# Queries and gates of a hybrid encoder layer: the tokens' high and low parts side by side in one matmul of 512 columns

## What is computed

```python
xn = rmsnorm(h, norm_g)
z = xn @ w_in                      # 2048 -> 3*1024 + 1024 + 1024 + 1024 + 3*1024 + 1024 + 3*2048
u, x1, x2 = short_conv(hy_in)      # width 3
y_a = hyena_mixer(u, x1, x2, kf, skip) * silu(hy_gate)      # two long convolutions by FFT
y_b = fourier_mixer(fn_in) * silu(fn_gate)                  # 2-D DFT, real part
y_c = neighborhood_attention(q, k, v, rpb, meta_bias) * silu(na_gate)
m = g_a * (y_a @ w_a) + g_b * (y_b @ w_b) + g_c * (y_c @ w_c)
out = rmsnorm(h + m @ w_out, final_g)[:, 16:]
```

## Time and profile before

| | us |
|---|---|
| median of 3 runs | 1137.92 |
| lowest and highest | 1137.79, 1138.51 |
| span of the profiled execution | 1136.7 |
| PE busy in it | 1111.2 |
| DVE busy | 767.9 |
| ACT busy | 567.7 |

### The profile page before, as it was taken

The page is one execution under the profiler, slowest core; times in us unless marked ns, Lnnn a source line. Parts: engine busy times, 40 slices in busy tenths (PEclk is TensorE's granted clock), DMA queues, the critical chain, the costliest instruction groups (busy, mean ns, idle before and its releaser), DMA issues.

```text
span 1136.7 us, 17224 instructions
## 1 busy us (share of the span) xinstructions
PE 1111.2 (98%) x7158; PEld 1006.8 (89%) x7158; DVE 767.9 (68%) x1149; ACT 567.7 (50%) x787; POOL 62.0 (5%) x98
## 2 busy tenths in 40 slices
PE   4999999999999999999999999999999999999997
PEld 2999999999999999999999988888888888888886
DVE  6778887778787687886888775454555455455554
ACT  6565555556545455554554564443444444344443
POOL 4030000300001200002000000000000000000000
PEclk9999999999999999999999999999999999999999
DMA  8644443644435533435543575555555555556652
GB/s 311 236 137 168 148 149 121 203 167 149 136 125 195 185 120 141 149 121 186 186 148 117 167 262 198 195 184 192 185 185 185 189 189 183 197 200 244 242 185 111
DMA packets 30494, 201.54 MB, mean 177 GB/s; under 512 B 3873, under 2 KB 4193, under 8 KB 7745
## 3 DMA queue, kind: packets, MB, share of 16 engines
q1 hardware_dynamic: 25024, 180.16, 45.3%
q0 software_dynamic: 5248, 19.77, 5.3%
q10 hardware_dynamic: 144, 0.52, 0.1%
HBM read 195.19 MB, written 5.24 MB: 176 GB/s over the span
## 4 chain that ended last, share of the span: by engine, by line
PE 74%; DVE 15%; ACT 6%; issue 4%; DMA 0%; ACTq 0%; DVEq 0%
PE ps L570 23%; PE ps L572 23%; PE ps L571 23%; DVE w_lo L1322 4%; ACT w_hi L982 2%; DVE prod L1563 1%; DVE prod L1564 1%; PE ps L594 1%; PE ps L575 1%; DVE k_lo L1322 1%; DVE prod L1565 1%; DVE y_lo L1322 1%; DVE prod L1566 1%; DVE hm L1409 1%; ACT y_hi L1183 1%
## 5 line engine op out<-in xcount | busy, mean ns | idle before, releaser
L1322 DVE TENSOR_TENSOR w_lo<-raw,w_hi 128x1024 fp32r<-128x1024 f32 x336 | 409.1, 1230 | 267.2 <-ACT w_hi L982 266.9
L982 ACT ACTIVATE w_hi<-raw 128x1024 fp32r<-128x1024 f32 x336 | 351.2, 1056 | 349.4 <-PE ps L572 347.6
L570 PE MATMUL ps<-xn_hi,w_hi 128*128 128x272 f32 (+2 forms) x1280 | 367.6, 287 | 0.0
L571 PE MATMUL ps<-xn_lo,w_hi 128*128 128x272 f32 (+2 forms) x1280 | 365.8, 286 | 0.0
L572 PE MATMUL ps<-xn_hi,w_lo 128*128 128x272 f32 (+2 forms) x1280 | 365.4, 285 | 0.0
L570 PEld LDWEIGHTS ps<-xn_hi,w_hi 128*128 128x128 f32 x1280 | 242.3, 189 | 2.0
L571 PEld LDWEIGHTS ps<-xn_lo,w_hi 128*128 128x128 f32 x1280 | 242.1, 189 | 0.7
L572 PEld LDWEIGHTS ps<-xn_hi,w_lo 128*128 128x128 f32 x1280 | 242.3, 189 | 0.0
L570 PE MATMUL ps<-w_hi,xn_hi 128*128 128x512 f32 x384 | 152.3, 397 | 0.0
L572 PE MATMUL ps<-w_hi,xn_lo 128*128 128x512 f32 x384 | 150.9, 393 | 0.0
L571 PE MATMUL ps<-w_lo,xn_hi 128*128 128x512 f32 x384 | 150.6, 392 | 0.0
(11 more groups left out here) (257 smaller groups left out, 1333.5 us busy)
## 6 DMA issues: line engine op xcount, KB each, us to landing
raw<-w_stream SPq DMA_DIRECT2D x168, 1024.0 KB, 4.9
branch_y<-ystage POOLq DMA_DIRECT2D x12, 256.0 KB, 3.3
y_raw<-branch_y POOLq DMA_DIRECT2D x3, 1024.0 KB, 6.7
xin<-x SPq DMA_DIRECT2D x2, 1024.0 KB, 6.9
w4s<-w POOLq DMA_DIRECT2D x16, 128.0 KB, 5.9
absd<-decay POOLq DMA_DIRECT2D x8, 256.0 KB, 6.3
h<-x POOLq DMA_DIRECT2D x2, 1024.0 KB, 8.0
rows_t<-rpb POOLq DMA_DIRECT2D x8, 219.0 KB, 6.2
```

The costliest lines, as they stand in the source:

```text
L570: mm(out_ap, a_hi, b_hi, start=first, stop=False)
L571: mm(out_ap, a_hi, b_lo, start=False, stop=False)
L982: A(w_hi[:, w % 2, part, :], raw[:, w % 4, 1024 * part:1024 * part + 1024], ACT.Copy).then_inc(hi_done, 1)
L1322: return V.tensor_tensor(dst, src, hi.bitcast(F32), ALU.subtract)
```

## The change

The two tiles `xn_hi` and `xn_lo` become halves of one tile `xn_two`. For q, hgate, ngate and fgate a new `summed_slab` replaces `proj_slab`: for each k one matmul with `w_hi` stationary and both parts of the 256 tokens moving, 512 columns into a whole bank (columns 0 to 255 w_hi*xn_hi, columns 256 to 511 w_hi*xn_lo), and one with `w_lo` stationary and xn_hi moving, 256 columns added to the first half. Two matmuls take the place of three. When the block ends, ACT copies the second half of the bank into an SBUF tile `both`, DVE adds the first half to it, and that frees the bank. What is made of the sum moves one slab on:

- q: both engines' work on `q_two` moves from step 3 to step 4, ahead of `spectra` on DVE;
- hgate: tanh and product from step 13 to step 14; ngate: from step 17 to step 18, with the product of branch c; fgate: from step 19 to step 0 of the next chunk;
- `fourier_gated` moves from step 19 to step 1 of the next chunk in chunks 1 to 3 (in chunk 0 it stands at step 1 in both).

```diff
+    xn_two = place("xn_two", [128, 2, KT, L], F32R)
+    xn_hi, xn_lo = xn_two[:, 0, :, :], xn_two[:, 1, :, :]
...
+    both = place("both", [128, 2, NG])
...
+            def summed_slab(w, bank, half):
+
+                for nt in range(2):
+                    pe.wait_ge(lo_done, 2 * w + nt + 1)
+                    for k in range(8):
+                        cols = slice(128 * k, 128 * k + 128)
+                        mm(ps[:, bank + nt, :].rearrange("p (h n) -> p h n", h=2), w_hi[:, w % 2, nt, cols],
+                           xn_two[:, :, 8 * half + k, NM:L], start=half == 0 and k == 0, stop=False)
+                        last = mm(ps[:, bank + nt, 0:NG], w_lo[:, w % 4, nt, cols], xn_hi[:, 8 * half + k, NM:L],
+                                  start=False, stop=half == 1 and k == 7)
+                    last.then_inc(half_used, 1)
...
# ACT
-                    ins = A(gate[:, :, :], src16, ACT.Tanh, scale=0.5)
+                    act.wait_ge(both_used, summed(c, name) - 1)
+                    A(both[:, :, :], ps[:, bank:bank + 2, NG:2 * NG], ACT.Copy).then_inc(half_kept, 1)
+                    return
...
+                    if t == 4:
+                        queries_high(c)
+                    if t in (14, 18):
+                        gate_tanh(c, "hgate" if t == 14 else "ngate")
+                    if t == 0:
+                        gate_tanh(c - 1, "fgate")
...
# DVE
+                if name in ("q", "hgate", "ngate", "fgate"):
+                    dve.wait_ge(half_kept, summed(c, name))
+                    V.tensor_tensor(both[:, :, :], both[:, :, :], ps[:, bank:bank + 2, 0:NG], ALU.add).then_inc(proj_read, 1)
+                    return
...
+            def gate_final(c, name):
+                dve.wait_ge(tanh_done, 3 * c + ("hgate", "ngate", "fgate").index(name) + 2)
+                V.scalar_tensor_tensor(gate[:, :, :], gate[:, :, :], 1.0, both[:, :, :], ALU.add, ALU.mult).then_inc(both_used, 1)
+                dve.wait_ge(both_used, summed(c, name))
...
-                    if t == 1 and c == 0:
-                        fourier_gated(0, 2)
+                    if t == 0:
+                        gate_final(c - 1, "fgate")
+                    if t == 1:
+                        fourier_gated(c)
                     if t == 4:
+                        queries_low(c)
                         spectra(c, (0, 1), 0)
+                    if t == 14:
+                        gate_final(c, "hgate")
...
-                    if t == 17:
+                    if t == 18:
+                        gate_final(c, "ngate")
...
-                    if t == 19 and c < LAST:
-                        fourier_gated(c + 1, blocks_read(c, "fgate"))
```

More of the change, by code:

```diff
@@ L102, in copies_made, with summed @@
 def copies_made(c, name):
-    return 1 + c * (NBLK - 2) + ("u", "q", "k", "x1", "x2", "hgate", "ngate", "fgate").index(name) + 1
+    return 4 * c + ("u", "k", "x1", "x2").index(name) + 1
+def summed(c, name):
+    return 4 * c + ("q", "hgate", "ngate", "fgate").index(name) + 2
 FPOS = np.concatenate([np.arange(256, L), np.arange(0, 256, 2), np.arange(1, 256, 2)])
@@ L803, in _ @@
                         wide_slab(slab_of(c, t), PAIR["gate", 0, 0], xn_hi, xn_lo, 4 * q, KT, NM)
+                    elif name in ("q", "hgate", "ngate", "fgate"):
+                        summed_slab(slab_of(c, t), 2 * (t // 2 % 2), t % 2)
                     else:
@@ L1128, in evac @@
                                 scale=params[:, bass.ds(c * 2 + (CW + 24 + t0 + i), 1)])
-                elif name == "q":
-                    for hh in range(HC):
-                        r = slice(64 * (hh % 2), 64 * (hh % 2) + 64)
-                        ins = A(q_two[r, hh, :].rearrange("p (r n) -> p r n", r=4),
-                                ps[r, bank + hh // 2, 0:NG].rearrange("p (r n) -> p r n", r=4)[:, :, ::-1], ACT.Copy, scale=0.125)
                 elif name == "k":
@@ L1147, in evac, with queries_high, gate_tanh @@
                 else:
[L1148 to L1154 removed]
+                    act.wait_ge(both_used, summed(c, name) - 1)
+                    A(both[:, :, :], ps[:, bank:bank + 2, NG:2 * NG], ACT.Copy).then_inc(half_kept, 1)
+                    return
+                ins.then_inc(a_ev, 1)
+            def queries_high(c):
+                act.wait_ge(proj_read, blocks_read(c, "q"))
+                for hh in range(HC):
+                    r = slice(64 * (hh % 2), 64 * (hh % 2) + 64)
+                    ins = A(q_two[r, hh, :].rearrange("p (r n) -> p r n", r=4),
+                            both[r, hh // 2, :].rearrange("p (r n) -> p r n", r=4)[:, :, ::-1], ACT.Copy, scale=0.125)
+                ins.then_inc(q_high, 1)
+            def gate_tanh(c, name):
+                act.wait_ge(proj_read, blocks_read(c, name) if c >= 0 else 2)
+                done, turns = {"hgate": (yb_done, c + 1), "ngate": (ya_done, c + 1), "fgate": (yc_done, c + 1)}[name]
+                if turns:
+                    act.wait_ge(done, turns)
+                if name == "hgate":
+                    act.wait_ge(s_mm, c * HC + HC)
+                A(gate[:, :, :], both[:, :, :], ACT.Tanh, scale=0.5).then_inc(tanh_done, 1)
             def turned(n_th, done, dst, rest, bank, ready, w=CC, twin=32):
@@ L1498, in evac @@
                 src = ps[:, bank:bank + 2, 0:L]
-                src16 = ps[:, bank:bank + 2, 0:NG]
                 if name == "v":
```

41 lines of the change are left out of this document (17 added, 24 removed).

## The result

The changed kernel takes 1156.7 us (median of 4 runs, 1156.0 to 1156.9); the kernel before took 1138.2 us in the runs beside it. The ratio is 1.0163, with a 95% interval of 1.0151 to 1.0176. So it is slower, as forecast, but by 18.5 us where 9.2 were forecast, and it lies above the range.

A forecast was written before the change was run, and what follows sets the result against it. PE was taken as the bound except where two DVE and ACT chains arrive late. Chain A 9.6, chain B 1.7 and PE -2.1 gave +9.2 us, 1147.1 us on the median of 1137.92; range 1140 to 1151.

The forecast's parts named there:

- What bounds the kernel: PE is the bound except where two chains of DVE and ACT make it wait, ahead of the scores and unfold.
- The gain on PE: Paired matmuls in q and gate slabs save 9.9 ns per contraction tile; -2.1 us where PE does not wait.
- fourier_gated and q in chain A: Added DVE and ACT work delays chain A: +0.69 us in chunks 1 to 3, +0.75 in all four.
- chain A: DVE and ACT work from step 1 to the scores after step 8; 3.19 us longer in chunks 1 to 3.
- POOL in chain A: Bias additions, now at step 1, collide with sd by turns: +1.75 us in chunks 1 to 3, bounds 0 to 2.5.
- tanh in chain B: ACT's later hgate tanh in step 14 delays unfold by 0.58 us in chunks 0 to 2, 1.7 us together.
- chain B: DVE and ACT work from the scores of step 11 to unfold, for which PE waits after step 16; +1.7 us.
- Elsewhere 0: Gate products of steps 18 and 0, branch c's later store and POOL's filter-weight loads cost 0 where PE is the bound.
- no collision: Rival: sd and make_bias pass each other or POOL starts later; +4.0 us, 1141.9 us; no or one collision, chance 0.20.
- dearer operand: Rival: 512 columns cost as much as two of 256, no PE gain; 1149.2 us; with a further wait, chance 0.13.

The follow-up runs named there:

- e1: The changed kernel with make_bias on POOL put ahead of the store of branch b; 1145.8 us, ratio 1.0070.
- e2: The kernel before with only fourier_gated of chunks 1 to 3 moved from step 19 to step 1 of the next chunk; 1151.9 us, ratio 1.0125.
- e18: The changed kernel with POOL's bias additions held until the product hm has been made; 1149.0 us, ratio 1.0100.
- e15: e2 with POOL's bias additions held until the product hm, just ahead of sd, has been made; 1143.3 us.
- e16: e2 with POOL's bias additions held until sd_lo of the same place has been made; 1147.1 us.
- e5: e1 with the tanh and product of hgate put back at step 13; 1142.1 us, ratio 1.0036.
- e12: e6 with the first branch's split put ahead of ngate's tanh and product in step 18 of the last chunk; 1134.8 us, ratio 0.9974.
- e9: e6 with each 512-column matmul split again into two of 256 columns; 1137.8 us, ratio 0.9998.
- e6: e5 with fourier_gated in step 0 of chunks 1 to 3 and the query subtractions put between the spectra's first steps; 1136.0 us, ratio 0.9983.
- e4: e1 with each 512-column matmul split again into two of 256 columns; 1146.6 us.
- e7: The changed kernel with 28 unused 256-column matmuls on PE ahead of its wait for the fold in chunks 1 to 3; 1155.7 us, ratio 1.0157.
- e8: e2 with POOL's bias additions held until the block of sd in question has been made; 1144.2 us.
- e11: e5 with fourier_gated made in step 0 of chunks 1 to 3; 1140.6 us, ratio 1.0026.

## Why the prediction was wrong in size

- **What bounds the kernel: right.** Both chains cost what was added to them. The warning against PE's 98% held: with PE's stream shorter, the time grew.
- **The gain on PE: right in kind, too large.** 9.9 ns per pair were predicted, 5 to 6 measured (2.79 instead of 2.84 us a half), since the pair takes 0.349 us and not 0.345: from the start of the 512-column matmul to the next it is 0.232 us in the median, where the merge has 0.227. Kept were 1.4 us instead of 2.1. The rows for 512 columns came from the merge, where the same kind of matmul follows; the prediction named as the bound and did not move toward it.
- **fourier_gated and q in chain A: right.** In chunk 1 PE waits 3.5 us for the fold, which is 0.69 + 3.35 less the 0.52 in hand. The two terms together were to cost 1.44 us a chunk; in e1, where no collision adds to them, they cost 1.2.
- **POOL in chain A: the step that failed.** Place, order and partner were right: `fourier_gated`, store, the four additions 0.16 us ahead of `sd`. The size was not: "`sd`'s first addition waits for POOL's first (0.95 us, 0.8 of it left), the second for POOL's second" made 1.75 us, and the trace has 3.35. With upper bound 2.5 it was outside the bounds too. The prediction took alternation from chunk 0 for a rule, where the worst case, the whole row of 3.64 us, was in the earlier trace rows. This is 1.6 x 3 = 4.8 of the 8.9 us that the span missed. e1, e2 and e18 show it by taking it away or putting it in; in e18 the row still meets `sd`, and with turns each chain A is 2.4 to 2.6 us shorter. Why this row lets DVE in only at its end, where the same row elsewhere takes turns, is open.
- The Trainium skill ("SBUF — State Buffer", "Who interferes with whom") says, of VectorE's modes that use two ports, that whoever issues first gets the shared pair for the whole instruction; it does not say who comes next. If the loser's turn is next, it waits for one addition, and in chunk 0, e15 and e16 the traces look so (0.90 to 1.97 us for an instruction of DVE, its own work included). `sd` of the changed kernel does not: it waits for four.
- **tanh in chain B: right.** 1.7 predicted, 2.1 measured; e5 took 1.5 us off the wait for `unfold`.
- **"Elsewhere 0": wrong by 1.3 us.** The same two hand-overs cost 0.4 us in step 15 of the last chunk (chain B's end, where I counted chunks 0 to 2 only) and 0.5 at the start of the merge, where the tanh of ngate now stands ahead of `yb_hi`; e12 undid the latter. q in chunk 0, taken as hidden (0 to 0.8), cost 0.35.
- **The clock: not in the prediction at all.** 1.4 us in chunk 0 and about 0.3 each in chunks 2 and 3 of the changed kernel.
- Rival "no collision" is what e1 tried: 1145.8, not 1141.9, since it still has the clock, the last chunk and the merge. Rival "dearer operand" came true in part: some 4 of the 9.9 ns are gone, and what is left still shows in e9. The range's upper end, 1151, had room for 1.3 us more of collision a chunk, not for the 1.6 of a full row.

## What to carry to other kernels

When an added hand-over delays one engine's instruction, look at what waits for it on the third engine, and price a collision at the whole row of instructions queued there, not at one of them. Work that a change adds to a busy-looking but not binding engine can be free, but only at the place where that engine waits: the same edit, with the same sums and copies, cost 18 us in the order it was given, and in another order, with POOL's row at another place, was 2 to 3 us faster than the kernel before (e6, e12). Before shortening PE's stream, find the chain that it hides.

## What the runs showed of the hardware

- A DVE addition of 0.42 us took 3.77 us beside four back-to-back POOL additions (also 4.04 for 512 elements), waiting for the last; other DVE instructions with two SBUF inputs took turns with the same POOL instructions and took 0.9 to 2 us each. For small ones the turn is most of it: 1.16 instead of 0.42, 0.90 instead of 0.17 us (e16).
- TensorE's granted clock fell from 1.00 to 0.5 (1.2 GHz) for 3.4 us behind waits of 1.2 us (e4), 1.4 (changed kernel, e1, e18), 2.2 (e16) and 3.5 us, not behind each of them. Filling the wait with matmuls kept it at 1.00 (e7). In e5, e6, e8, e11 and e12, whose longest waits in the chunks are 0.9 to 1.3 us, it did not fall before the end. So the length of the wait alone does not tell.
- A 512-column matmul whose moving operand is two pieces of 256 from two places, followed by one of 256, takes 0.349 us; three of 256 take 0.355. Over the program that is 1.8 us (e9 against e6), known to some 1.4 us.
